# Sample queries stationary, keys copied, value products moved: the attention stage of a decoder step

## The chip, the cores and the metric

The kernel runs on one core of a Trainium2 chip. The metric is device time in microseconds of one execution, lower is better.

## The reference

One inference step of a one-layer hybrid decoder: 16 meta tokens and 256 prompt tokens, and 8 sample tokens with their caches, 280 rows of 1024 features. All in float32.

```python
h = rmsnorm(x, norm_mix)
xr, q, k, v, g_rnn, g_attn = split_in(h, w_in)         # 16 heads of 64, 2 kv heads
y_rnn = rg_lru(causal_conv(xr), w_rg, w_ig, lam)       # gates in 16 blocks of 64 x 64, a scan over the tokens
y_attn = window_attend(q, k, v, ...)                   # window 128, ALiBi slopes, a sink per head
x = x + concat(sigmoid(g_rnn) * y_rnn, sigmoid(g_attn) * y_attn) @ w_out
x = x + moe(rmsnorm(x, norm_ffn), ...)                 # top 4 of 32 experts, clamped SwiGLU
y = rmsnorm(x, norm_final)
...
# outputs: y, the last 128 keys and values, the convolution and scan states
```

The sample rows attend to their 127 cached keys and the new one, each row to its own cache.

## The kernel before, in words

Each engine runs a program written out by hand; order is that of the code, and semaphores tie the engines together. There are two stages.

**Trunk.** Everything is held feature-major: partitions are features, columns are the 280 tokens. TensorE goes through 34 projection blocks n (128 output features, eight matmuls over the 1024 inputs, line 1055): 0 and 1 are keys and values, 2 to 9 the recurrent branch, 10 to 17 the queries (BLK_Q), then the two sets of gates. Four PSUM banks and later two take the blocks in turn; ScalarE evacuates each (line 621). Between blocks TensorE does the small work:

- after_kv (line 939): keys and values are transposed to token-major, VectorE copies them (token_major, line 1445) into kt4, with each key head twice, and vt. keys_major (line 947, after block 4) transposes the doubled keys back, so that kd holds each kv head's keys in both halves of the partitions; ScalarE evacuates them (line 645). The halves are needed since queries of two heads lie in the two halves.
- gates(j) (line 954), after block j + 3: four 64 x 64 matmuls in four quarters of the array into banks 4 and 5; ScalarE takes them with three sigmoids (gate_evacs, lines 625 and 629). VectorE's convolution of block j must come first, GpSimd multiplies behind them.
- From step 0 (st, block ATT = 15) on, head pairs j = 0 to 7: scores(j) at st = 2j+1 (line 914), the softmax on VectorE and ScalarE, p_transposes(j) at st = 2j+3 (line 923), pv(j), the value products, at st = 2j+4 (lines 934 and 936), and ScalarE's evacuation of pv(j) right after (line 712).
- The 16 prompt tokens of the third tile (last rows) and the 8 sample rows have products of their own: last_scores and sample_scores at st 9 (lines 981 and 972), sample_rows at st 11 (line 987; it turns the sample scores so that rows are (sample, head)), last_p and sample_p at st 14, sample_pv at st 15 (line 1007), last_pv at st 16 (lines 1017 and 1018).

Matmuls name their part of the array by the partitions of operands and output: 64-row operands use half of its rows, 64-partition outputs half of its columns, and so on. This is what "tile size" means here.

After step 18 follow eight output blocks (line 1100), the router, and the experts.

**Experts.** 16 pairs of experts, 12 weight loads of 2 MB each, through ten places of SBUF. SyncE issues them (lines 432 and 436) as places come free: the first wait for attn_gated and bias_step, that is for VectorE's last gating of attention outputs (line 1646) and the split of the expert biases (lines 1651 to 1657); some of the ten places belong to trunk weights and wait for output blocks (wout_used). TensorE does the pairs with lines 1319 and 1355.

```python
elif 4 <= st <= 2 * KB + 2:
    pv((st - 4) // 2)                                   # line 1069
...
if st >= 4 and st % 2 == 0 and st <= 2 * KB + 2:        # line 709, ScalarE
    jj = (st - 4) // 2
    eng.wait_ge(s.pv_done, jj + 1)
    act(m_t[:, KB + jj, 0:2 * P], bank[5][:, 0:2 * P], ACT.Copy).then_inc(s.pv_evac, 1)
```

## Time and profile before

| what | value |
| --- | --- |
| median of 3 runs | 1148.07 us (1147.6 to 1148.33) |
| profiled execution: span from first to last instruction | 1146.0 us |
| TensorE busy | 1113.5 us, 97% |
| VectorE, ScalarE, GpSimd busy | 311.8, 229.6, 34.0 us |
| HBM read | 436.00 MB, 383 GB/s over the span |
| granted TensorE clock, mean | 0.999 |

The profile is of one execution. Its own time outside the profiler isn't recorded; beside the span stands the median of the runs, 2.07 us above it. The trace gives for each instruction its engine, line, start and duration; matmuls overlap, so the time of a group is read from one group's start to the next one's. A float32 matmul shows as two records.

### The profile page before, as it was taken

The numbers are of one execution on the slowest core, as the hardware profiler recorded it, in microseconds if no ns is written. First come the engines' busy times: TensorE is split into PE (matmuls) and PEld (weight loads), VectorE is DVE, ScalarE is ACT, GpSimd is POOL, SyncE is SP. The second block draws the span as 40 slices with busy tenths as digits, with TensorE's granted clock in tenths as the row PEclk, the third lists the DMA queues.
The fourth block names the chain that finished last, engine by engine and source line by source line (L and its number), as shares of the span: only waits on it lengthen the run. The fifth ranks groups of instructions, "written<-read, shape, count | busy, mean of one in ns | idle before, by whom it ended". The sixth has DMA issues, their size and how long they took to land.

```text
span 1146.0 us, 14903 instructions
## 1 busy us (share of the span) xinstructions
PE 1113.5 (97%) x5772; PEld 493.6 (43%) x5772; DVE 311.8 (27%) x785; ACT 229.6 (20%) x642; POOL 34.0 (3%) x69
## 2 busy tenths in 40 slices
PE   8999999999999999999999999999999999999997
PEld 6687778844333424333333333323232323232432
DVE  5665544032131221212130312121213030312123
ACT  4564363422020202010101111111111101010103
POOL 0200012210000000000000000000000000000000
PEclk9999999999999999999999999999999999999999
DMA  9743636989999999999999999999999999999995
GB/s 350 265 153 111 187 112 265 426 350 421 427 428 426 426 427 428 428 428 428 427 428 428 430 429 428 427 428 429 429 429 427 427 428 429 429 427 427 426 427 238
DMA packets 40802, 437.90 MB, mean 382 GB/s; under 512 B 6720, under 2 KB 9040, under 8 KB 11072
## 3 DMA queue, kind: packets, MB, share of 16 engines
q1 hardware_dynamic: 40136, 435.65, 91.2%
q10 hardware_dynamic: 624, 1.68, 0.4%
q8 instruction: 28, 0.46, 0.2%
q14 instruction: 14, 0.11, 0.0%
HBM read 436.00 MB, written 2.41 MB: 383 GB/s over the span
## 4 chain that ended last, share of the span: by engine, by line
PE 69%; DMA 24%; DVE 3%; ACT 2%; issue 1%; DVEq 0%; SPq 0%; ACTq 0%
PE bank L1319 21%; DMA ring<-in_w_down 20%; PE bank L1355 19%; PE bank L1055 8%; PE bank L1100 5%; PE bank L1201 4%; DMA area<-in_w_down 3%; PE bank L1222 3%; PE bank L1150 2%; PE bank L1235 1%; PE bank L1198 1%; PE bank L1036 1%; PE bank L1225 1%; DVE area L1748 1%; PE bank L923 1%
## 5 line engine op out<-in xcount | busy, mean ns | idle before, releaser
L1319 PE MATMUL bank<-ring,area 128*64 128x512 f32 x1744 | 396.4, 597 | 9.1 <-DMA ring<-in_w_up 8.7
L1319 PEld LDWEIGHTS bank<-ring,area 128*64 128x64 f32 x1744 | 117.2, 136 | 261.8 <-issue 222.9
L1355 PE MATMUL bank<-ring,area 128*64 128x512 f32 x928 | 213.7, 599 | 7.5 <-DMA ring<-in_w_down 7.5
L1736 DVE TENSOR_TENSOR x_tok<-x_tok,bank 128x512 f32<-128x512 f32 x60 | 41.3, 688 | 328.0 <-PE bank L1222 328.0
L800 ACT ACTIVATE area<-area 128x256 f32<-128x256 f32 x64 | 26.7, 417 | 516.3 <-DVE area L1748 516.3
L1055 PE MATMUL bank<-ring 128*128 128x264 f32 (+1 forms) x512 | 121.7, 393 | 0.0
L1355 PEld LDWEIGHTS bank<-ring,area 128*64 128x64 f32 x928 | 62.4, 136 | 117.9 <-issue 102.7
L1055 PEld LDWEIGHTS bank<-ring 128*128 128x128 f32 x512 | 95.2, 190 | 21.3 <-issue 4.0
L1773 DVE TENSOR_TENSOR area<-area 128x1024 f32<-128x1024 f32 x15 | 18.4, 1225 | 211.3 <-ACT area L810 211.3
L1222 PE MATMUL bank<-area 128*128 128x512 f32 x128 | 71.8, 644 | 0.0
L1319 PE MATMUL bank<-area 128*64 128x512 f32 x304 | 69.2, 597 | 1.5 <-DMA area<-in_w_up 1.5
L1100 PE MATMUL bank<-area,ring 128*128 128x264 f32 x256 | 58.6, 387 | 0.0
L1201 PE MATMUL bank<-area,h_tok 128*128 128x128 bf16 x768 | 54.2, 219 | 0.0
L1100 PEld LDWEIGHTS bank<-area,ring 128*128 128x128 f32 x256 | 48.0, 190 | 8.8 <-issue 1.0
L810 ACT ACTIVATE area<-bank,vec 128x128 f32<-128x128 f32 x120 | 34.3, 369 | 82.5 <-PE bank L1201 82.5
L1201 PEld LDWEIGHTS bank<-area,h_tok 128*128 128x128 bf16 x768 | 48.9, 98 | 0.0
L1748 DVE TENSOR_SCALAR area<-bank 128x256 f32<-128x256 f32 x64 | 26.9, 420 | 74.1 <-PE bank L1319 74.1
L1222 PEld LDWEIGHTS bank<-area 128*128 128x128 f32 x128 | 19.1, 188 | 51.6 <-issue 51.6
L1319 PEld LDWEIGHTS bank<-area 128*64 128x64 f32 x304 | 20.5, 136 | 45.2 <-issue 39.2
L820 ACT ACTIVATE area<-bank 128x512 f32<-128x512 f32 x32 | 19.1, 597 | 80.9 <-PE bank L1235 80.9
L1198 PE MATMUL bank<-area,h_tail 72*128 72x128 bf16 x128 | 28.5, 223 | 0.0
L1752 DVE SCALAR_TENSOR_TENSOR area<-area 128x256 f32<-128x256 f32 x64 | 27.2, 425 | 2.2
(271 smaller groups left out, 702.6 us busy)
## 6 DMA issues: line engine op xcount, KB each, us to landing
ring<-in_w_up SPq DMA_DIRECT2D x103, 2048.0 KB, 34.3
ring<-in_w_down SPq DMA_DIRECT2D x51, 2048.0 KB, 33.9
area<-in_w_up SPq DMA_DIRECT2D x17, 2048.0 KB, 29.8
ring<-in_w_in SPq DMA_DIRECT2D x16, 1024.0 KB, 9.3
ring<-in_w_down SPq DMA_DIRECT2D x13, 1024.0 KB, 10.6
ring<-in_w_up SPq DMA_DIRECT2D x12, 1024.0 KB, 9.7
area<-in_w_down SPq DMA_DIRECT2D x5, 2048.0 KB, 34.3
ring<-in_w_out SPq DMA_DIRECT2D x8, 1024.0 KB, 5.0
```

Of the source, the lines that this page charges most:

```text
L800: act(sig[:, n % 2, :], glu[:, n % 2, :], ACT.Sigmoid, scale=ALPHA).then_inc(s.sig_ready, 1)
L810: ins = act(xe[:, j, :], bank[half][:, P * i:P * (i + 1)], ACT.Copy, scale=vec[:, NFF + j:NFF + j + 1])
L1055: m = mm(proj_bank(n)[:, 0:T - lo], w[:, k, P * (n % 2):P * (n % 2) + P], (xn if n == 2 else h_t)[:, k, lo:T], start=(k == 0), stop=(k == ...
L1100: mo = mm(bank[m % 2][:, 0:NT], w[:, k, :], m_t[:, k, N_META:T], start=(k == 0), stop=(k == 2 * KB - 1))
L1198: mm(out, h_tail[0:TRIO, P * j:P * (j + 1)], g_oh[0:TRIO, 2, :], start=True, stop=False)
L1201: m = mm(out, parts[:, t, i, P * j:P * (j + 1)], g_oh[:, t, :], start=False, stop=(t == 1 and i == 2))
L1222: m = mm(b[:, :], gw_t[:, lo:lo + P], yd[:, NB * c:NB * (c + 1)], start=True, stop=True)
L1319: m = mm(bank[2 * h + n][64 * e:64 * e + 64, :], xe[:, k, 64 * e:64 * e + 64], w[:, kk, e, NB * n:NB * (n + 1)], start=False, stop=(k == K ...
L1355: m = mm(bank[4 + c][64 * e:64 * e + 64, :], y_t[:, 4 * half + f, 64 * e:64 * e + 64], w[:, f, e, :], start=False, stop=(half == 1 and f = ...
L1736: eng.tensor_tensor(x, x, combined_bank(unit, last)[:, :], ALU.add).then_inc(s.added, 1)
L1748: eng.tensor_scalar(glu[:, n % 2, :], z[:, :, 0], LIMIT, None, ALU.min).then_inc(s.glu_ready, 1)
L1752: eng.scalar_tensor_tensor(out=lin[:, n % 2, :], in0=lin[:, n % 2, :], scalar=1.0, in1=glu[:, n % 2, :], op0=ALU.add, op1=ALU.mult).then_i ...
```

## The change

1. keys_major goes. kt4 holds each key head once, token_major makes four copies and not six. kd is filled from kv_t by copies: GpSimd the halves whose partitions are their own (kd_own), ScalarE the crossed ones (kd_ready).
2. gates run by the table GATES: pairs (0, 1), (2, 3), (4, 5) after blocks 4, 6 and 8, gates 6 and 7 after blocks 9 and 10 as before. Odd gates use banks 6 and 7. ScalarE's evacuations follow the same table.
3. pv(j) moves from st = 2j+4 to st = 2j+5, between scores(j+2) and p_transposes(j+1); pv(7) stays at st 18. ScalarE evacuates pv(j) at st = 2j+6, and pv(6) and pv(7) both at st 18.
4. sample_scores: the queries are the stationary operand, 32 columns for each of four column tiles (four samples by eight query heads, the rest of the 16 zero for the other kv head), the cached keys move. The result has its rows where the softmax wants them; sample_rows and VectorE's copy s_t go. VectorE lays the queries out with eight copies and not four. Sample rows are now ordered by (sample mod 4, sample div 4, head).
5. last_pv does its four matmuls of 128 rows first and then its four of 16 rows.

```diff
+GATES = ((), (), (0, 1), (), (2, 3), (), (4, 5), (6,), (7,))
...
-                    eng.wait_ge(s.kd_ready, 2)
...
-                    eng.wait_ge(s.kvtok_ready, 6)
+                    eng.wait_ge(s.kvtok_ready, 4)
...
+            eng.wait_ge(s.zeroed, 10)
+            eng.wait_ge(s.kv_evac, 1)
+            for kv in range(N_KV):
+                half = slice(64 * kv, 64 * kv + 64)
+                eng.tensor_copy(kd[half, kv, :], kv_t[half, 0, :]).then_inc(s.kd_own, 1)
+                eng.wait_ge(s.kd_own, kv + 1)
...
+                    eng.wait_ge(s.kv_evac, 1)
                     for kv in range(N_KV):
-                        eng.wait_ge(s.kd_tr, kv + 1)
-                        act(kd[:, kv, :], bank[6 + kv][:, 0:T], ACT.Copy).then_inc(s.kd_ready, 1)
-                if j >= 1:
-                    gate_evacs(j - 1)
+                        there, here = slice(64 - 64 * kv, 128 - 64 * kv), slice(64 * kv, 64 * kv + 64)
+                        act(kd[there, kv, :], kv_t[here, 0, :], ACT.Copy).then_inc(s.kd_ready, 1)
+                for i in GATES[j]:
+                    gate_evacs(i)
...
-                if st >= 4 and st % 2 == 0 and st <= 2 * KB + 2:
-                    jj = (st - 4) // 2
-                    eng.wait_ge(s.pv_done, jj + 1)
-                    act(m_t[:, KB + jj, 0:2 * P], bank[5][:, 0:2 * P], ACT.Copy).then_inc(s.pv_evac, 1)
+                if st >= 6 and st % 2 == 0 and st <= 2 * KB + 2:
+                    for jj in range((st - 6) // 2, (st - 4) // 2 if st < 2 * KB + 2 else KB):
+                        eng.wait_ge(s.pv_done, jj + 1)
+                        act(m_t[:, KB + jj, 0:2 * P], bank[5][:, 0:2 * P], ACT.Copy).then_inc(s.pv_evac, 1)
...
             def p_transposes(j):
+                if j == 0:
+                    eng.wait_ge(s.gate_evac, 3 * KB)
...
-                if j:
-                    eng.wait_ge(s.gate_evac, 3 * j)
+                if j > 1:
+                    eng.wait_ge(s.gate_evac, 3 * (j - 1))
+                elif j == 1:
+                    eng.wait_ge(s.kvtok_ready, 4)
...
-                qd = qdz.rearrange("p k (g b) -> p k g b", g=GROUP)
-                for b in range(B_S):
-                    m = mm(bank[4][:, N_HEADS * b:N_HEADS * (b + 1)], kc_t[:, b, :], qd[:, :, :, b], start=True, stop=True)
+                for g in range(2):
+                    for i in range(4):
+                        r = slice(32 * i, 32 * i + 32)
+                        m = mm(bank[4][r, 0:P], qdz[:, g, r], kc_t[:, 4 * g + i, :], start=(g == 0), stop=(g == 1),
+                               skip_group_check=True)
...
-                for kv in range(N_KV):
-                    v = slice(HEAD * kv, HEAD * (kv + 1))
-                    for p in range(2):
-                        o, r = slice(64 * p, 64 * p + 64), slice(64 * p, 64 * p + 64)
-                        mm(bank[4][o, 64 * kv:64 * kv + 64], vt[:, 1, v], pt_2[:, kv, r], start=True, stop=False)
-                        m = mm(bank[4][o, 64 * kv:64 * kv + 64], vt[0:TAIL_P, 2, v], pt_2[0:TAIL_P, 2 + kv, r],
-                               start=False, stop=True)
+                for n, t in ((P, 1), (TAIL_P, 2)):
+                    for kv in range(N_KV):
+                        for p in range(2):
+                            r = slice(64 * p, 64 * p + 64)
+                            m = mm(bank[4][r, 64 * kv:64 * kv + 64], vt[0:n, t, HEAD * kv:HEAD * (kv + 1)],
+                                   pt_2[0:n, kv + (t - 1) * N_KV, r], start=(t == 1 and kv == 0), stop=(t == 2),
+                                   skip_group_check=True)
...
-                {2: after_kv, 4: keys_major}.get(n, lambda: None)()
+                {2: after_kv}.get(n, lambda: None)()
...
                     if st < 2 * KB:
                         scores(st // 2)
+                    if st >= 5:
+                        pv(st // 2 - 2)
                     if st >= 3:
                         p_transposes(st // 2 - 1)
-                elif 4 <= st <= 2 * KB + 2:
-                    pv((st - 4) // 2)
+                elif st == 2 * KB + 2:
+                    pv(KB - 1)
```

How the instructions move. TensorE, blocks 3 to 6 of the trunk, before (1055 are projection blocks, 963 gates, 951 the transposes of the keys):

```order
L1055 MATMUL bank<-ring 128x280 x8
L963 MATMUL bank<-ring,h_tok 64x280 x4
L1055 MATMUL bank<-ring 128x280 x8
L951 MATMUL bank<-keep,area 128x128 x2
L951 MATMUL bank<-keep,area 128x24
L951 MATMUL bank<-keep,area 128x128 x2
L951 MATMUL bank<-keep,area 128x24
L963 MATMUL bank<-ring,h_tok 64x280 x4
L1055 MATMUL bank<-ring 128x280 x8
L963 MATMUL bank<-ring,h_tok 64x280 x4
L1055 MATMUL bank<-ring 128x280 x8
L963 MATMUL bank<-ring,h_tok 64x280 x4
```

and with the change (1063 are the projection blocks, 973 the gates):

```order
L1063 MATMUL bank<-ring 128x280 x16
L973 MATMUL bank<-ring,h_tok 64x280 x8
L1063 MATMUL bank<-ring 128x280 x16
L973 MATMUL bank<-ring,h_tok 64x280 x8
```

Two blocks stand together, then two gates; the key transposes are gone. TensorE, one head pair's turn in the attention part, before (914 scores, 923 transposes of probabilities, 934 and 936 value products):

```order
L914 MATMUL bank<-area,ring 128x128 x2
L914 MATMUL bank<-area,ring 128x256 x2
L923 MATMUL bank<-keep,area 128x128 x6
L1055 MATMUL bank<-ring 128x264 x8
L934 MATMUL bank<-area 64x256 x2
L936 MATMUL bank<-area 64x128 x2
L1055 MATMUL bank<-ring 128x264 x8
```

and with the change (927, 949 with 951, 938):

```order
L927 MATMUL bank<-area,ring 128x128 x2
L927 MATMUL bank<-area,ring 128x256 x2
L949 MATMUL bank<-area 64x256 x2
L951 MATMUL bank<-area 64x128 x2
L938 MATMUL bank<-keep,area 128x128 x6
L1063 MATMUL bank<-ring 128x264 x16
```

The value products stand where TensorE is away from the full array anyway. ScalarE, its last instructions of the trunk with their waits, before (706 evacuates transposed probabilities, 712 value products):

```order
L621 ACTIVATE ring<-bank 128x264 [waits proj_done]
L706 ACTIVATE area<-bank 128x384 [waits pv_done,pt_done]
L621 ACTIVATE ring<-bank 128x264 [waits proj_done]
L712 ACTIVATE area<-bank 128x256 [waits pv_done]
L743 ACT_TABLE_LOAD
```

and with the change (718 and 724):

```order
L629 ACTIVATE ring<-bank 128x264 [waits proj_done]
L718 ACTIVATE area<-bank 128x384 [waits pv_done,pt_done]
L629 ACTIVATE ring<-bank 128x264 [waits proj_done]
L724 ACTIVATE area<-bank 128x256 [waits pv_done] x2
L755 ACT_TABLE_LOAD
```

Both of the last two value products are now evacuated behind the last projection block.

## Rows read from the trace of the kernel before

**Rows 1.** Windows: us, busy of each engine (x instructions), granted clock, DMA share, GB/s.

```profile
235.00:240.00 5.00, 4.79 (x37) 2.47 (x37) 2.01 (x6) 2.70 (x6) 1.45 (x4) 1.00 0.64 269
...
250.00:255.00 5.00, 5.00 (x36) 2.26 (x36) 2.63 (x9) 0.00 (x0) 0.00 (x0) 1.00 1.02 426
```

**Rows 2.** Chain of work that ended last: start us, us, what.

```profile
399.56 7.02 PE bank L1319 x32
...
454.52 7.02 PE bank L1319 x32
...
790.60 39.28 DMA ring<-in_w_down
...
849.33 39.29 DMA area<-in_w_down
```

**Rows 3.** Waits of SyncE's queue, 150 to 330 us: total us, times, longest.

```profile
SPq L436 <- PE bank L1100: 15.0, 2, 7.9
SPq L441 <- DVE bias_parts L1657: 13.3, 1, 13.3
```

**Rows 4.** TensorE's timeline, first probability transposes: start us, us, line, operation [idle before].

```profile
89.00 0.92 PE L923 MATMUL bank<-keep,area 128*128 128x128 f32 x6 [0.43 <-DVE area L1553]
```

**Rows 5.** TensorE's timeline, trunk blocks, key transposes and gates.

```profile
28.82 1.09 PE L951 MATMUL bank<-keep,area 128*128 128x128 f32 x6
29.84 0.70 PE L963 MATMUL bank<-ring,h_tok 64*64 64x280 f32 x8
30.48 4.04 PE L1055 MATMUL bank<-ring 128*128 128x280 f32 x16
...
35.08 4.04 PE L1055 MATMUL bank<-ring 128*128 128x280 f32 x16
...
57.88 21.66 PE L1055 MATMUL bank<-ring 128*128 128x264 f32 x96
```

**Rows 6.** Timelines of ScalarE, VectorE and GpSimd beside the gates.

```profile
25.25 1.28 ACT L625 ACT_TABLE_LOAD   x1
...
35.98 1.01 ACT L629 ACTIVATE ring<-bank,vec 64x280 f32<-64x280 f32 x2
...
35.60 0.50 DVE L1481 SCALAR_TENSOR_TENSOR ring<-ring,vec 128x272 f32<-128x272 f32 x1 [1.67 <-ACT ring L638]
...
37.37 0.74 DVE L1483 SCALAR_TENSOR_TENSOR ring<-ring,vec 128x8 f32<-128x8 f32 x1
...
28.15 0.77 POOL L545 TENSOR_TENSOR ring<-ring 128x280 f32<-128x280 f32 x1 [25.62 <-ACT ring L629]
```

**Rows 7.** Timelines of TensorE and VectorE, one turn of the attention part.

```profile
99.53 3.73 PE L1055 MATMUL bank<-ring 128*128 128x264 f32 x16
...
107.75 0.93 PE L914 MATMUL bank<-area,ring 64*128 64x128 f32 x8
...
109.32 3.73 PE L1055 MATMUL bank<-ring 128*128 128x264 f32 x16
...
104.82 0.34 DVE L1553 TENSOR_SCALAR area<-area 128x256 f32<-128x256 f32 x1
```

**Rows 8.** TensorE's timeline, sample scores and sample value products.

```profile
119.91 1.94 PE L972 MATMUL bank<-area,h_tok 128*128 128x16 f32 x16
121.70 3.81 PE L1055 MATMUL bank<-ring 128*128 128x264 f32 x16
...
151.72 1.10 PE L1007 MATMUL bank<-area 128*64 128x8 f32 x32
```

**Rows 9.** TensorE's timeline, the last rows' value products, first and the block behind.

```profile
157.21 0.28 PE L1017 MATMUL bank<-area 128*64 128x64 f32 x2
...
159.21 3.83 PE L1055 MATMUL bank<-ring 128*128 128x264 f32 x16
```

**Rows 10.** ScalarE's timeline, the last block and the last value products.

```profile
167.29 0.39 ACT L621 ACTIVATE ring<-bank 128x264 f32<-128x264 f32 x1 [3.40 <-PE bank L1055]
168.10 0.38 ACT L712 ACTIVATE area<-bank 128x256 f32<-128x256 f32 x1 [0.42 <-PE bank L936]
```

More of the change, by code:

```diff
@@ L356, in msk, with gate_banks @@
             return masks[:, lo - C_KEEP:lo - C_KEEP + n]
+        def gate_banks(j):
+            return bank[4 + 2 * (j % 2)], bank[5 + 2 * (j % 2)]
         def proj_bank(n):
@@ L623, in gate_evacs @@
             def gate_evacs(j):
+                r_bank, i_bank = gate_banks(j)
                 eng.wait_ge(s.gate_done, 2 * j + 1)
-                act(a_t[:, j, :], bank[4][:, 0:T], ACT.Sigmoid, bias=vec[:, BR + j:BR + j + 1]).then_inc(s.gate_evac, 1)
+                act(a_t[:, j, :], r_bank[:, 0:T], ACT.Sigmoid, bias=vec[:, BR + j:BR + j + 1]).then_inc(s.gate_evac, 1)
                 eng.wait_ge(s.gate_done, 2 * j + 2)
@@ L628, in gate_evacs @@
                     here, there = slice(64 * h, 64 * h + 64), slice(64 - 64 * h, 128 - 64 * h)
-                    act(b_t[there, j, :], bank[5][here, 0:T], ACT.Sigmoid, bias=vec[here, BI + j:BI + j + 1])\
+                    act(b_t[there, j, :], i_bank[here, 0:T], ACT.Sigmoid, bias=vec[here, BI + j:BI + j + 1])\
                         .then_inc(s.gate_evac, 1)
@@ L688, in _ @@
                 if n == BLK_Q:
-                    gate_evacs(KB - 1)
+                    for i in GATES[KB]:
+                        gate_evacs(i)
                 elif n < BLK_Q + 3:
@@ L945, in after_kv @@
                     tr.then_inc(s.kv_tr, 1)
-            def keys_major():
-                eng.wait_ge(s.kvtok_ready, 6)
-                for kv in range(N_KV):
-                    for t, (lo, n) in enumerate(TILES):
-                        tr = eng.transpose(bank[6 + kv][:, lo:lo + n], kt4[0:n, t, P * kv:P * (kv + 1)], ident[0:n, 0:n])
-                    tr.then_inc(s.kd_tr, 1)
             def gates(j):
@@ L962, in gates @@
                         c, half = h if g == 0 else 1 - h, slice(64 * h, 64 * h + 64)
-                        m = mm(bank[4 + g][64 * c:64 * c + 64, 0:T], wg[half, g, j, :], xc[half, j, :],
+                        m = mm(gate_banks(j)[g][64 * c:64 * c + 64, 0:T], wg[half, g, j, :], xc[half, j, :],
                                start=True, stop=True, tile_position=(64 * h, 64 * c))
@@ L982, in last_scores @@
                            start=True, stop=True)
-            def sample_rows():
-                eng.wait_ge(s.dsc_ready, 1)
-                eng.wait_ge(s.x_biased, 2)
-                eng.transpose(bank[4][:, 0:P], s_t, ident).then_inc(s.dst_done, 1)
             def sample_p():
@@ L1057, in _ @@
                 m.then_inc(s.proj_done, 1)
-                {2: after_kv, 4: keys_major}.get(n, lambda: None)()
+                {2: after_kv}.get(n, lambda: None)()
                 if BLK_XR + 1 <= n < BLK_Q + 1:
-                    gates(n - BLK_XR - 1)
+                    for j in GATES[n - BLK_XR]:
+                        gates(j)
                 st = n - ATT
@@ L1448, in token_major @@
                     src = bank[6 + i][:, 0:3 * P].rearrange("p (t k d) -> p t k d", t=3, k=N_KV)
-                    for dup in range(2 - i):
-                        dst = (kt4.rearrange("p t (k r d) -> p t k r d", k=N_KV, r=2)[:, :, :, dup, :] if i == 0
-                               else vt.rearrange("p t (k d) -> p t k d", k=N_KV))
-                        eng.tensor_copy(dst[:, 0:2], src[:, 0:2]).then_inc(s.kvtok_ready, 1)
-                        eng.tensor_copy(dst[0:TAIL, 2], src[0:TAIL, 2]).then_inc(s.kvtok_ready, 1)
+                    dst = (kt4, vt)[i].rearrange("p t (k d) -> p t k d", k=N_KV)
+                    eng.tensor_copy(dst[:, 0:2], src[:, 0:2]).then_inc(s.kvtok_ready, 1)
+                    eng.tensor_copy(dst[0:TAIL, 2], src[0:TAIL, 2]).then_inc(s.kvtok_ready, 1)
             def softplus():
@@ L1618, in _ @@
                         for p in range(2):
-                            eng.tensor_copy(qdz[64 * kv:64 * kv + 64, kv, :].rearrange("p (i r b) -> p i r b", i=4, r=2)[:, :, p, :],
-                                            q_t[64 * p:64 * p + 64, 4 * kv:4 * kv + 4, L:T]).then_inc(s.qd_ready, 1)
+                            for g in range(2):
+                                own = qdz[64 * kv:64 * kv + 64, g, :].rearrange("p (b h) -> p h b", b=4)
+                                h = N_HEADS * g + GROUP * kv + p
+                                eng.tensor_copy(own[:, h:h + GROUP - 1:2, :],
+                                                q_t[64 * p:64 * p + 64, 4 * kv:4 * kv + 4, L + 4 * g:L + 4 * g + 4])\
+                                   .then_inc(s.qd_ready, 1)
                     attention_sum(j)
```

23 lines of the change are left out of this document (10 added, 13 removed).

## The prediction

> **What bounds the kernel now.** I read four views. First the windows: between 250 and 255 us TensorE is busy all the time and the DMA engines are too, at 426 GB/s, while between 235 and 240 us they move only 269 GB/s [rows 1]. The reader should see that the transfers dip once, where the expert stage begins. Second the chain of work that ended last: until about 730 us an expert pair costs TensorE 54.95 us (454.52 - 399.56 = 54.96), later it repeats every 58.73 us (849.33 - 790.60) and each turn ends on a weight transfer [rows 2]. So the weight stream is the slower of the two from its start; TensorE only works off its lead. Third the waits of the DMA queue between 150 and 330 us: its first expert load waits 13.3 us for VectorE's bias pieces (the chain attention outputs, gating, bias split), and the eleventh, in two halves, waits 15.0 us for TensorE's last output blocks [rows 3]. Fourth TensorE's timeline: before the expert stage it has no idle time worth naming after 15 us except 0.43 us before the first probability transposes [rows 4].
>
> Put together: the end is the time at which the stream becomes steady plus a fixed amount of bytes. That time hangs on TensorE's output blocks and first expert loads, which hang on TensorE's own trunk. A microsecond taken from TensorE before 168 us therefore moves the end by one microsecond, as long as VectorE's attention chain (which releases the first loads) moves as well. No later cover hides it: TensorE's spare time after 730 us is of no use, but the stream's start is.
>
> **The change part by part.** The profiled span is 1146.0 us and the median of the runs 1148.07, so 2.07 us lie around the span; I treat them as fixed and subtract from the median.
>
> 1. **Key transposes out.** Line 951's six transposes go: 29.84 - 28.82 = 1.02 us [rows 5]. The keys are now copied inside SBUF: ScalarE makes two half copies in place of two from PSUM, about the same, and GpSimd two more near 18 us, in a stretch where it waits (25.62 us before 28.15) [rows 6], long before the first scores. VectorE loses two copies (about 0.5 us) before its second convolution. SP's wait for kvtok_ready 4 in place of 6 and the dropped kd_ready wait can only release it earlier. **-1.0.**
>
> 2. **Gates in pairs.** A projection block with its gates repeats every 35.08 - 30.48 = 4.60 us. A block alone takes 21.66/6 = 3.61 us for 264 columns, so 3.83 for 280; the gates cost 0.77. One matmul of 280 columns streams in 3.83/8 = 0.48; the four gate matmuls lie in four quarters of the array and can run side by side, so 0.48 is work and about 0.29 is the change of tile size there and back [rows 5]. Three visits go: **-0.9** (bounds 0 and -0.9).
>
> 3. **What pairing makes late.** ScalarE's gate evacuations (0.50 us each, three for a gate) now come six in a row, the first time with the 1.28 us table load and the two key copies in front. Block 4 ends near 28.1 us in the new order (28.82 less the gates that leave block 3). From there I add 0.2 for the signal, four copies of 0.45 (the block's two and the keys'), 1.28 and 6 x 0.50: 34.4 us before block 5's evacuation, and 1.0 more until its convolution can start, which took 2.5 us on VectorE (35.60 to 38.11): 37.9. TensorE, with 3.9 us for a block and 1.25 for a pair of gates, wants it for gates(3) at 37.5. The later pairs follow a block that had no gates in front of it, with 0.7 us to spare by the same sum. I take **+0.25** (0 to 0.5) [rows 6].
>
> 4. **Value products between scores and transposes.** A turn of two blocks lasts 109.32 - 99.53 = 9.79 us. Two blocks alone are 2 x 3.61 = 7.22, scores and transposes 109.32 - 107.75 = 1.57: the value products account for 1.00, of which 384 columns' streaming, 0.65, is work (their two halves lie side by side) [rows 5, 7]. The other 0.35 is at most 0.17 for each of two changes of tile size; rows 9 say 0.14. Between scores (64-row tiles) and transposes (full array) only one more change is needed. Six heads' pairs: 6 x 0.14 = **-0.8** (0 to 6 x 0.35 = -2.1). pv(6) is counted in 6. Nothing new is late: VectorE's next pt copy waits 0.4 us for the later transposes, and the probabilities, ready at 105.16, are wanted after the scores that start at 107.75.
>
> 5. **Sample scores with queries stationary.** Eight matmuls now cost 121.70 - 119.91 = 1.79 us, 0.11 per weight load record, for almost no columns. The new ones stream 8 x 128 columns in four column tiles: 0.22 us each, two rounds of four, 0.44 if they run side by side as the value products do, 1.75 if not. Small stationary tiles load fast here: the sixteen sample value matmuls took 1.10 us for 32 records. With two changes 0.75: **-1.0** (0 to -1.3). The rows' transpose (about 0.15, a sixth of the 0.92 us of six [rows 4]) and VectorE's copy go too, **-0.1** [rows 8]. VectorE's four more query copies, some 0.2 us each, lie where over 3 us are spare [rows 7].
>
> 6. **Last rows by tile size.** Eight matmuls alternate between 128-row and 16-row tiles: 159.21 - 157.21 = 2.00 us, 0.25 each, of which 64 columns stream in 0.11: 0.14 per change, the best single price of a change here [rows 9]. Grouped, two rounds of each kind take 4 x 0.11, and with the change between them 0.58. But pv(6) no longer stands in front in the same tile size, so it needs two changes of its own and this group one more: 0.28 to 0.42. 2.00 - 0.58 - 0.42 = **-1.0** (-0.6 to -1.4).
>
> 7. **The last value products wait.** This is the added wait. pv(7) stays after the last block and needs pv(6)'s bank evacuated. ScalarE did that a block earlier; now its order is evacuation of block 33, then pv(6), then pv(7). The first takes 0.39, the second 0.38, and a signal of about 0.1 lies ahead of and behind them: TensorE stands about 0.95 us before pv(7). Behind it on TensorE is the first output block; VectorE waits for the same evacuation with the last two gatings (before: 167.29 and 168.10) and then the bias split that releases the first loads [rows 10]. **+0.95** on both chains.
>
> Sum: -1.0 - 0.9 + 0.25 - 0.8 - 1.0 - 0.1 - 1.0 + 0.95 = -3.6 us. Both chains end on TensorE's last blocks, so the first loads and the first expert pair move together and the dip of rows 1 keeps its shape. 1148.07 - 3.6 = **1144.5 us**.
>
> Against the change speaks a rule of the Trainium skill (SBUF — State Buffer, Terms): VectorE and GpSimd share a port pair, and the loser "fully blocks". By that rule GpSimd's two key copies hold VectorE's normalizing and first convolutions up by their own length; taking one of its full products of 280 columns (0.77 us) for the pair's bound, the stall of term 3 would grow to 1.0 and the sum be -2.85, 1145.2 us. No row before shows the collision, since GpSimd waits in that stretch.
>
> **The rivals.**
>
> *Changes of tile size are not the cost* (13%). If the 0.14 to 0.29 us beside the streaming belong to weight loads or issue, which move along, terms 2, 4 and half of 6 vanish: -1.0 - 1.0 - 0.1 - 0.5 + 0.95 + 0.25 = -1.4, so 1146.7. For it: each of those matmuls has a weight load of its own. Against: rows 9, where the same small matmuls cost 0.25 alternating, and 16 sample matmuls in one tile size only 0.07 each [rows 8].
>
> *The scan chain keeps its time* (8%). The 0.43 us idle before the first transposes shows that ScalarE's and VectorE's chain from gates(7) to the first probabilities already ends last there. If the pairs delayed gates(7)'s evacuation by what TensorE gained (terms 1 to 3, 1.65 us), TensorE would wait that much longer and the time is 1148.07 - 1.95 = 1146.1. Against: gates 6 and 7 stay single, and the last pair's six evacuations (3.0 us) end before the next block does.
>
> *Everything at its good bound* (15%): terms 2, 4, 5 and 6 at -0.9, -2.1, -1.3, -1.4, no stall in 3: -1.1 - 0.9 - 2.1 - 1.3 - 1.4 + 0.95 = -5.85, so 1142.2.
>
> *Slower: TensorE's clock falls after the new pause* (4%). The 0.95 us stand before pv(7) follows small tiles. If the granted clock went from 2.4 to 1.2 GHz for one output block (16 matmuls, twice the 3.61 us of a projection block [rows 5]), that block would take 7.2 us more: 1144.5 + 7.2 = 1151.7. It decides once more than half an output block runs at the lower level. Against: the granted clock is 1.00 in the windows, also around the dip, where TensorE had short waits. The Trainium skill (TensorE: Matmul & The Clock Gate, Part 1) has the throttled state as the default that activity releases; by that rule the time is this rival's, if the pause is enough, and no row here shows one that was.
>
> **How the numbers follow.** The forecast itself has 60%, with 1143.4 to 1145.7 as its own range (terms 3 to 6 between neighbouring bounds). From the cases: faster by over 0.2% (below 1145.8; about what a measurement of this kernel can tell from no change) is the forecast and the good bound, 75%; within 0.2% the two rivals with 1146.7 and 1146.1, 21%; slower 4%. The range of 8 in 10 reaches from 1142.7 to 1146.8: it takes in the two rivals and most of the way to the good bound, and leaves out the slower case and the tails.
>
> **What would show it.** In the profile after: no transposes of keys; block pairs with gates about 0.3 us shorter per pair; turns of two blocks near 9.65 us; sample scores under 0.8 us; the last rows near 0.6 us; an idle time of about 0.9 us before the last value products, ended by ScalarE; the first expert load near 177.4 us and not 181.0, and the last weight landing near 1115. A wait of TensorE for the convolution at the second gate pair over 0.5 us makes term 3 wrong; sample scores near 1.8 us makes term 5 wrong. The whole is wrong if TensorE reaches the first output block 3.6 us earlier and the end does not follow, or if a granted clock below 1.00 appears.

## The result, and the profile after

The changed kernel takes 1150.24 us (median of 14 runs), the kernel before on the same chip 1147.52 us (14 runs): a ratio of 1.002, 95% interval 1.0012 to 1.0028. The change makes the kernel 2.7 us slower, where 3.6 us less were forecast. One of the 14 runs of the changed kernel was a slow one, 2902.27 us, and is left out of the ratio (the median without it is 1150.19). The profiled execution took 1150.52 us, with a span of 1148.7 us and a mean granted clock of 0.985 (before 1146.0 us and 0.999).

The trunk did what was forecast, and a little more. TensorE's timeline of the changed kernel, in the places of [rows 5], [rows 7], [rows 8] and [rows 9] (start us, us, line, operation, idle before it and what ended it):

```profile
20.25 7.71 PE L1063 MATMUL bank<-ring 128*128 128x280 f32 x32
27.89 1.18 PE L973 MATMUL bank<-ring,h_tok 64*64 64x280 f32 x16
28.99 7.81 PE L1063 MATMUL bank<-ring 128*128 128x280 f32 x32
36.74 1.28 PE L973 MATMUL bank<-ring,h_tok 64*64 64x280 f32 x16
37.95 7.81 PE L1063 MATMUL bank<-ring 128*128 128x280 f32 x32
...
97.26 7.29 PE L1063 MATMUL bank<-ring 128*128 128x264 f32 x32
...
106.85 7.29 PE L1063 MATMUL bank<-ring 128*128 128x264 f32 x32
...
117.33 0.64 PE L983 MATMUL bank<-h_tok,area 128*32 128x128 f32 x16
117.90 7.39 PE L1063 MATMUL bank<-ring 128*128 128x264 f32 x32
...
152.18 0.83 PE L1025 MATMUL bank<-area 128*64 128x64 f32 x16
152.94 3.83 PE L1063 MATMUL bank<-ring 128*128 128x264 f32 x16
...
162.78 0.65 PE L949 MATMUL bank<-area 128*64 128x256 f32 x4 [0.85 <-ACT area L724]
163.23 0.42 PE L951 MATMUL bank<-area 128*64 128x128 f32 x4
163.58 6.72 PE L1109 MATMUL bank<-area,ring 128*128 128x264 f32 x29
```

A pair of gates stands for 28.99 - 27.89 = 1.10 us (the second for 37.95 - 36.74 = 1.21), a turn of two blocks lasts 106.85 - 97.26 = 9.59 us instead of 9.79 [rows 7], the sample scores take 0.57 us instead of 1.79, the last rows 0.76 instead of 2.00, and the new wait is there with 0.85 us. The first output block starts at 163.58 us (before 167.99), the first expert matmul at 233.04 (before 237.44), and the first expert load is issued at 176.61 us (before 181.02): 4.4 us earlier, all three.

Then it is lost again. The page of the changed kernel, the lines that differ: the granted clock, the queue over which code is fetched, and the chain of work that ended last.

```profile
PEclk9999999999999999989999989999999999999999
...
q8 instruction: 55, 0.90, 0.3%
...
PE 90%; DVE 4%; issue 3%; ACT 2%; DMA 0%; DVEq 0%; SPq 0%; ACTq 0%
```

Before, q8 had 28 packets and 0.46 MB, and the chain was TensorE 69%, DMA 24%. TensorE's waits in the changed kernel (us in total, times, longest):

```profile
PE bank L1328 <- issue: 8.7, 3, 3.3
PE bank L1159 <- issue: 8.4, 3, 3.1
```

Neither row is in the answer for the kernel before, whose longest waits there are for weights. They fall at three places, about 504, 679 and 854 us. TensorE's timeline at the first of them:

```profile
500.48 3.65 PE L1364 MATMUL bank<-ring,area 128*64 128x512 f32 x16
506.85 1.03 PE L1159 MATMUL bank<-bias_parts,chosen 96*128 96x512 bf16 x4 [2.71 <-issue]
507.81 1.12 PE L1328 MATMUL bank<-area 128*64 128x512 f32 x1
512.21 6.08 PE L1328 MATMUL bank<-area 128*64 128x512 f32 x14 [3.28 <-issue]
```

L1159 are bias matmuls, here those with which a pair begins. TensorE's code for twelve of the sixteen pairs is a loop of three pairs, run four times; each of the three places is its jump back. TensorE waits twice for no other engine and no weight, and the windows around it (us, busy of each engine, granted clock, DMA share, GB/s) show that the work behind, 14 records in 6.08 us where 16 take 3.65 elsewhere, runs at a lower clock:

```profile
500.00:510.00 10.00, 6.22 (x31) 2.03 (x29) 1.83 (x3) 2.23 (x6) 0.00 (x0) 0.89 1.01 428
510.00:520.00 10.00, 7.79 (x24) 3.23 (x25) 0.00 (x0) 0.00 (x0) 0.00 (x0) 0.60 0.99 418
...
513.00:515.00 2.00, 2.00 (x8) 0.94 (x6) 0.00 (x0) 0.00 (x0) 0.00 (x0) 0.50 1.02 434
```

In windows of 2 us the granted clock is 0.50, the lower level of 1.2 GHz, from 509 to 517 us: it fell between 507 and 509 (0.69), behind the first wait, and came back between 517 and 519 (0.75), while TensorE worked.

In every third pair the bias matmuls ahead of its second half start at 264.91, 429.87, 604.80, 779.34 and 953.95 us: 164.96 us for three pairs without a jump, 174.93, 174.54 and 174.61 with one. Each jump back costs 9.6 to 10.0 us in this kernel, 29.2 together.

### The profile page after: what moved, and what is told of

Same layout as the page of the kernel before. It is cut to its first block, busy times and chain, and to the rows that moved or that the text cites. A ratio compares the mean times of both kernels' runs of the same rounds, so it can differ in the third digit from the quotient of the medians.

```text
span 1148.7 us, 14892 instructions
## 1 busy us (share of the span) xinstructions
PE 1116.1 (97%) x5765; PEld 496.5 (43%) x5765; DVE 310.8 (27%) x786; ACT 229.3 (20%) x642; POOL 34.6 (3%) x71
## 4 chain that ended last, share of the span: by engine, by line
PE 90%; DVE 4%; issue 3%; ACT 2%; DMA 0%; DVEq 0%; SPq 0%; ACTq 0%
PE bank L1328 36%; PE bank L1364 20%; PE bank L1063 8%; PE bank L1231 6%; PE bank L1109 5%; PE bank L1210 4%; PE bank L1159 2%; PE bank L1244 2%; PE bank L1234 1%; DVE area L1757 1%; DVE area L1769 1%; PE bank L1207 1%; PE bank L1044 1%; PE bank L938 1%; ACT area L812 1%
## 5 line engine op out<-in xcount | busy, mean ns | idle before, releaser
L1328 PE MATMUL bank<-area 128*64 128x512 f32 x304 | 79.6, 652 | 8.7 <-issue 8.7
L1328 PEld LDWEIGHTS bank<-area 128*64 128x64 f32 x304 | 24.7, 148 | 57.2 <-issue 56.9
L1159 PE MATMUL bank<-bias_parts,chosen 96*128 96x512 bf16 x96 | 27.8, 401 | 8.4 <-issue 8.4
```

Of the source, the lines that this page charges most:

```text
L1159: mm(bank[b0 + n - n0][:, :], chosen[:, :], bias_parts[:, NB * n:NB * (n + 1)], start=True, stop=False, skip_group_check=True)
L1328: m = mm(bank[2 * h + n][64 * e:64 * e + 64, :], xe[:, k, 64 * e:64 * e + 64], w[:, kk, e, NB * n:NB * (n + 1)], start=False, stop=(k == K ...
```

## The experiments

**Where the loop's code lies.** The program's instruction list says where this comes from. A transpose is two instructions, so the seven removed ones (six of keys, one of sample rows) put everything behind them 14 instructions earlier; the waits added and removed cancel. The loop is 1767 instructions long. With q8's 0.46 MB in 28 packets a fetch is 16.4 KB, and in the first pass through the loop (330 to 505 us) the kernel before makes seven, 252 instructions each. The Trainium skill (Runtime: NRT & Kernel Launch, Instruction fetch mechanics) gives pieces of 256 instructions, and a store of 2048 instructions for TensorE that is filled first in, first out. It also has a jump stall on a fetch when its target isn't in the current window of two pieces. The traces agree with the store and not with the window: in the kernel before each jump goes back over nearly seven pieces (1767 of 7 x 256 instructions), and q8 has no packet for it (below). Counted in pieces of 256, the loop begins at place 195 of its piece before the change and at 181 after (up to a constant: what is put ahead of the program when it is loaded isn't in the list). Theory A: at 181 the loop crosses one piece more, the store no longer holds it with the piece fetched ahead, and each jump back starts fetching all of it anew. Theories B and C were the rivals: the stalls come with the change's timing, or with its new pause and the clock.

a_plus14 gives the loop of the changed kernel its old place back, b_minus14 takes it from the kernel before, and a_plus40 and b_plus40 move both on by 40.

```diff
 a_plus14, changed kernel (a_plus40: 20 in place of 7; b_plus40: 20, in the kernel before)
             keep_warm(14, bank[7])
+            for _ in range(7):
+                mm(bank[7][:, 0:8], ones[:, :], ones[:, 0:1].to_broadcast([P, 8]), start=True, stop=True)
 b_minus14, kernel before
-            keep_warm(14, bank[7])
+            keep_warm(7, bank[7])
```

> Edit: the changed kernel with 7 matrix products of 8 columns (14 TensorE instructions) more in its warm-up, so that TensorE's loop over the expert pairs begins at the same place in its instruction stream as in the kernel before. Theory A (the place of the loop's code: moved 14 instructions towards the start, its 1767 instructions lie across one more 16 KB piece of the code, and at each of the three loop-backs the code is fetched again): no waits on issue of over 1 us in the expert stage, 28 packets on the instruction queue q8 as before the change, granted clock back at 1.00 per 100 us there, 1143.2 us, from 1142.5 to 1144.2 (1147.5 less the 4.4 us that the trunk gained). Theory B (the loop-back stalls come with the change's own timing: weights that arrive earlier, so that a fetch of code meets a fuller DMA, or TensorE comes to the loop-back in another phase): three stalls of some 6 us and 55 packets remain, 1149 to 1151 us. Theory C (the clock falls because of the 0.85 us pause ahead of the last value product, and the rest follows): clock 0.6 behind the loop-backs remains, 1148 to 1151 us.

> Edit: the changed kernel with 20 matrix products of 8 columns (40 TensorE instructions) more in its warm-up: the loop begins 26 instructions behind the place that it has in the kernel before. Theory A: 1767 instructions fit into seven pieces of 256 only from the first 26 places of a piece, so whatever the exact offset (unknown, since what the runtime puts ahead of the program is not in the program), this one lies across eight pieces again: three stalls, 55 packets on q8, 1149 to 1153 us. If instead seven or eight pieces make no difference and only the piece in which the loop's first instruction lies counts, no stalls, about 1144. Theories B and C: stalls as in the changed kernel, 1149 to 1153 us.

> Edit: the kernel before with 7 warm-up products instead of 14 (14 TensorE instructions less), nothing else: the loop begins where it does in the changed kernel. Theory A: three waits on issue of 2.5 to 3.5 us twice each at the loop-backs around 507, 682 and 857 us, 55 packets on q8, granted clock 0.6 for 10 us behind each; of some 30 us lost there, what the stream of weights doesn't hide remains: 1151 to 1157 us. Theories B and C: the kernel before has none of the change's timing, so no stall in its loop, 28 packets; 1147 to 1149 us, the later end for a colder clock at the start.

> Edit: the kernel before with 20 matrix products of 8 columns (40 TensorE instructions) more in its warm-up, nothing else. Theory A: offset over 25 in its piece of 256, so eight pieces, three stalls at the loop-backs, 55 packets on q8, 1151 to 1157 us. Theories B and C: 28 packets, no stall, 1147 to 1150 us (up to 2 us for the longer warm-up).

| kernel | loop begins at place | us (before 1147.74) | ratio, 95% interval | packets on q8 |
| --- | --- | --- | --- | --- |
| a_plus14 | 195 | 1143.29 | 0.9964 (0.9951 to 0.9978) | 28 |
| a_plus40 | 221 | 1143.39 (one run) | | 28 |
| b_minus14 | 181 | 1157.06 | 1.0084 (1.0069 to 1.01) | 55 |
| b_plus40 | 235 | 1153.43 (one run) | | 55 |

Fourteen instructions more, idle products of 0.3 us, take 7 us off the changed kernel (1150.24 to 1143.29, the profiled span from 1148.7 to 1140.8); fourteen fewer put 9.3 us on the kernel before. In a_plus14 TensorE has no wait on issue left, and the chain ends on the weights again; page and waits of **a_plus14**:

```profile
q8 instruction: 28, 0.46, 0.2%
...
PE 70%; DMA 24%; DVE 3%; ACT 2%; issue 1%; DVEq 0%; SPq 0%; POOL 0%; POOLq 0%
```

```profile
PE bank L1330 <- DMA ring<-in_w_up: 8.9, 35, 0.4
PE bank L1366 <- DMA ring<-in_w_down: 7.5, 11, 0.8
```

The longest waits of **b_minus14**, which has nothing of the change:

```profile
PE bank L1319 <- issue: 11.1, 3, 3.9
PE bank L1150 <- issue: 8.5, 3, 2.9
```

and of **b_plus40**:

```profile
PE bank L1152 <- issue: 10.9, 3, 3.7
```

So B and C fall: the stalls come and go with the place alone, in either kernel. One expectation of A fell with them. By the count 1767 instructions fit into seven pieces from 26 places in a row, and 195 and 221 are 26 apart, so at most one of them should have been free of stalls unless the count is off by one; both are. The runs bound the good stretch: at least the 27 places 195 to 221, and not 181 nor 235, so between one place in ten (27 of 256) and one in five (53); the kernel before stood on a good one. b_minus14 came out just beyond the end of its range since its colder start costs too: its output blocks start at 169.85 us, 1.9 later. So of its 9.3 us some 1.9 aren't the loop's.

What the place does to the fetches is seen in the queues' packets (queue: packets, MB, share). **Kernel before**, 330 to 505 us, the loop's first pass; in the next 175 us q8 has no packet at all:

```profile
q8 instruction: 7, 0.11, 0.3%
```

**Changed kernel**, 505 to 680 us, the second pass:

```profile
q8 instruction: 9, 0.15, 0.3%
```

Nine fetches in each of three passes are the 27 packets more. That agrees with the Trainium skill's first in, first out (same section): once the first piece is overwritten, each piece that is fetched drives out the next one needed.

The price of a jump depends on the place too. By the same bias matmuls it is 8.6, 8.9 and 9.1 us in b_minus14, and 5.4, 5.4 and 6.3 in b_plus40, which waits on issue once per jump and not twice.

**Is it the jump or the fetching?** Written out, the loop has nearly the same fetches and no jump.

```diff
 unrolled, on a_plus14
-            with eng.Fori(0, TURNS // (TRIPLE * PAIR_LOADS)) as it:
+            for it in range(TURNS // (TRIPLE * PAIR_LOADS)):
 peel_first: turn 0 written out, then Fori(1, ...); 40 small products in the warm-up
 peel_last:  Fori(0, ... - 1), then turn 3 written out
```

> Edit: the changed kernel (with the 14 warm-up instructions more) with TensorE's loop over the twelve middle pairs written out, so that TensorE takes no jump back; 5301 instructions more in the program, which are fetched in any case. Theory A, sharpened (a store of eight pieces of 256 instructions, one piece fetched ahead; what costs is a jump back to a piece that has been overwritten, not the fetching): about 28 + 21 = 49 packets on the instruction queue q8, nearly as many as in the changed kernel, but no wait on issue and no fall of the clock; 1143.3 us, from 1142.5 to 1144.3. Theory D (27 more code fetches of 16 KB disturb the weight stream or TensorE wherever they fall): 1146 to 1150 us, with waits on issue or on weights in the expert stage.

It took 1147.75 us (ratio 0.9999, 0.999 to 1.0009), with 48 packets on q8. A was half right and half wrong. The jump is what stalls TensorE: no wait on issue and no low clock is left. But twenty fetches aren't free. From the first expert matmul to the end the written-out kernel takes 1145.5 - 232.46 = 913.0 us, a_plus14 1140.8 - 232.18 = 908.6: 4.4 us. The time is in waits for weights, longest 2.0 and 1.2 us where a_plus14 has 0.8 and 0.4; waits of **unrolled**:

```profile
PE bank L1330 <- DMA ring<-in_w_up: 10.1, 36, 1.2
PE bank L1366 <- DMA ring<-in_w_down: 8.0, 10, 2.0
```

I took from this that a fetch costs something only from about 760 us on, where TensorE's lead is used up (theory E), and not wherever it falls (D). One turn written out, early or late, tells the two apart.

> Edit: the changed kernel with the first of the four turns of TensorE's loop written out ahead of the loop, and 40 products of 8 columns in the warm-up, so that the loop over the other three begins at place 200 of a piece of 256 (places 195 and 221 left no stall). Seven more pieces of code are fetched (35 packets on q8), all of them before 560 us, where TensorE keeps its full pace and the weights wait for it. Theory E (the fetches of the written-out kernel cost their 4.5 us where the stream of weights is the bound, from about 760 us on, since each holds up one weight transfer; before that they are free): no cost, 1143.6 us (1142.6 to 1144.6, the longer warm-up in it). Theory D (each extra fetch costs some 0.22 us wherever it falls): 7 x 0.22 = 1.6 us, 1145.

> Edit: the changed kernel with the 14 warm-up instructions more and the last of the four turns of TensorE's loop written out behind the loop: six or seven more fetches, between 760 and 940 us, where the weights are the bound. Theory E: waits for weights of over 1 us once or twice, 1145.3 us (1144.3 to 1147). Theory D: 1.6 us, 1144.9 (which this run alone doesn't tell from E; peel_first does). If neither, and the written-out kernel was slow for another reason (its jump-free waits, its fetches late in the program): 1143.3.

**peel_first**, with seven fetches more between 507 and 657 us, took 1144.78 us (0.9976, 0.9967 to 0.9985), **peel_last**, with six more between 843 and 976 us, 1144.53 (0.9975, 0.9966 to 0.9984). From the first expert matmul to the end that is 1142.7 - 233.04 = 909.7 and 1142.3 - 232.3 = 910.0 us, so 1.0 and 1.4 us more than a_plus14: 0.15, 0.23 and (unrolled) 0.22 us per fetch, early or late. D holds and E falls. In peel_first the early fetches cost late: from the bias matmuls at 264.91 us to those at 704.87 it is 0.2 us behind a_plus14, from there to those at 1114.32 another 0.9. The weight stream never pauses, and what a fetch takes from it is missed when the lead is gone. These differences are small, but the eight kernels with 28 packets all take 908.6 to 908.9 us for this stage. In peel_first the loop begins seven pieces later in the program, at place 200 of its piece, and doesn't stall either, so it is the place within a piece that counts. Why 16 KB, 0.04 us at 428 GB/s, cost four to six times that wasn't tried.

The kernels that stall have both costs, and the larger one decides. b_plus40 loses 5.4 + 5.4 + 6.3 = 17.1 us at its jumps, less than TensorE has to spare (21.5 us, worked out below), and from 945 us on it waits for weights again. Yet its expert stage takes 1151.6 - 237.15 = 914.5 us, 5.9 more than the kernel before: 0.22 us for each of its 27 fetches. b_minus14 is also 5.8 us longer there (1153.7 - 239.30 = 914.4). So the fetches alone would have taken back more than the trunk's 4.4 us (an estimate from these runs; no run has the changed kernel's fetches without its stalls).

**The trunk, part by part.** The start of the kernel varies by up to 1.0 us from one profile to another, so I measure from projection block 3 (which the expectations call the third) to the first output block. **Kernel before**:

```profile
20.38 3.94 PE L1055 MATMUL bank<-ring 128*128 128x280 f32 x16
...
167.99 4.27 PE L1100 MATMUL bank<-area,ring 128*128 128x264 f32 x18
```

That is 147.61 us before; 143.33 in the changed kernel, and 143.28, 143.29 and 143.30 in a_plus14, a_plus40 and unrolled. Each experiment below is an edit of a_plus14, with the loop at the same place.

```diff
 pv7_bank: the last value products in another PSUM bank
-                eng.wait_ge(s.pv_evac, j)
+                if j < KB - 1:
+                    eng.wait_ge(s.pv_evac, j)
+                vb = bank[5 if j < KB - 1 else 2]
 (and vb for bank[5] in the products and in ScalarE's copy)
 pairs_undone
-GATES = ((), (), (0, 1), (), (2, 3), (), (4, 5), (6,), (7,))
+GATES = ((), (0,), (1,), (2,), (3,), (4,), (5,), (6,), (7,))
 pv_back: pv((st - 4) // 2) at every even st from 4 on, ScalarE's copy in the same turn
 rows_undone: last_pv as before the change
 pv7_pair: pv7_bank, and the table's end (4, 5), (), (6, 7))
```

> Edit: the changed kernel with the 14 warm-up instructions more, and the last turn's value products written to PSUM bank 2, which is free by then, instead of bank 5, so that they don't wait for ScalarE's copy of the product before. If the 0.85 us wait at 162.8 us is a term of its own (+0.95 in the forecast): the first output block starts 0.8 us earlier, 1142.5 us against 1143.3. If ScalarE's copy, not TensorE, sets the end of the attention stage there: the wait moves to the output block's wait for the gated rows, 1143.3 us.

> Edit: the changed kernel with the 14 warm-up instructions more, and each turn's value products back in their own place behind the second projection block of the turn, with ScalarE's copy one turn earlier as before the change; the wait of the last products for the copy goes with it. By the forecast (-0.8 for eight turns, +0.95 for the wait): 0.15 us faster than 1143.3, 1143.15. By the trace of the changed kernel (0.20 less in each of seven turns, 0.85 wait): 0.55 us slower in the turns less 0.85, so 1143.0 (1142.7 to 1143.4). If tile-size changes cost nothing: 0.85 faster, 1142.45.

> Edit: the changed kernel with the 14 warm-up instructions more, and the gates one at a time again, one behind each projection block of the stage. By the forecast's terms (pairs save 0.9, ScalarE's double turn costs 0.25): 0.65 us slower than 1143.3, so 1143.95 (1143.6 to 1144.3); by the trace of the changed kernel (stage shorter by 1.96, of which the key transposes 1.0): 0.96 slower, 1144.25. Rival: switches between products of 128 rows and of 64 cost nothing, and the stage was shortened by the banks in turn: 1143.2 to 1143.4.

> Edit: the changed kernel with the 14 warm-up instructions more, and the sixteen-row queries' value products back in their order before the change (two products of 128 rows and of 16 rows in turn, four times). By the forecast's term 6: 1.0 us slower, 1144.3; by the trace of the changed kernel: 1.24 slower, 1144.5, and 1.24 more from the third projection block to the first output block (143.28 with the change). Rival (changes of tile size aren't what cost time): no more than 0.2 slower, 1143.3 to 1143.5.

Each ratio is to the kernel before on the same chip, whose medians are 1147.57 to 1147.99 us.

| kernel | us | ratio to before, 95% interval | block 3 to output block |
| --- | --- | --- | --- |
| a_plus14 | 1143.29 | 0.9964 (0.9951 to 0.9978) | 143.28 |
| pv7_bank | 1142.71 | 0.9953 (0.9939 to 0.9967) | 142.37 |
| pv_back | 1143.37 | 0.9959 (0.9943 to 0.9975) | 143.13 |
| pairs_undone | 1144.99 | 0.9974 (0.9963 to 0.9984) | 144.72 |
| rows_undone | 1144.51 | 0.9974 (0.9964 to 0.9984) | 144.60 |

*pv7_bank*: the wait is gone, and nothing took its place, 0.91 us. In the timeline of **pv7_bank** the products follow the block with no idle time:

```profile
158.72 3.28 PE L1066 MATMUL bank<-ring 128*128 128x264 f32 x14
161.93 0.65 PE L952 MATMUL bank<-area 128*64 128x256 f32 x4
162.41 0.39 PE L954 MATMUL bank<-area 128*64 128x128 f32 x4
162.73 6.50 PE L1112 MATMUL bank<-area,ring 128*128 128x264 f32 x28
```

*pv_back* has no such wait either, so against pv7_bank it is the place of the value products alone: 0.76 us. The seven moved products don't share this evenly. **pv_back**, from the block after the first transposes to the block before pv(6), and from there to the last block:

```profile
87.83 3.73 PE L1065 MATMUL bank<-ring 128*128 128x264 f32 x16
...
149.62 3.83 PE L1065 MATMUL bank<-ring 128*128 128x264 f32 x16
...
159.10 3.73 PE L1065 MATMUL bank<-ring 128*128 128x264 f32 x16
```

and **pv7_bank**:

```profile
87.75 7.29 PE L1066 MATMUL bank<-ring 128*128 128x264 f32 x32
...
148.40 3.83 PE L1066 MATMUL bank<-ring 128*128 128x264 f32 x16
...
158.27 3.73 PE L1066 MATMUL bank<-ring 128*128 128x264 f32 x16
```

Six turns are 61.79 - 60.65 = 1.14 us shorter with the move, 0.19 each; pv(6), which had stood beside the last rows' products of the same tile size, costs 9.87 - 9.48 = 0.39. The expectation from the trace had 0.20 for all seven and took the wait off twice, so it missed. Against a_plus14 its trunk is 0.15 us shorter, as the forecast's terms had it, and its time 0.1 us longer, which these intervals can't tell from 0.15 shorter. The move was thus worth almost nothing with the wait that it brought.

*pairs_undone* is 1.44 us longer in the trunk, more than the 0.96 expected. Of this 0.37 is a wait that only this kernel has, for the first convolution, since gate 0 now comes a block earlier. Timeline of **pairs_undone**:

```profile
20.33 3.94 PE L1065 MATMUL bank<-ring 128*128 128x280 f32 x16
24.64 0.70 PE L975 MATMUL bank<-ring,h_tok 64*64 64x280 f32 x8 [0.37 <-DVE ring L1492]
25.27 4.04 PE L1065 MATMUL bank<-ring 128*128 128x280 f32 x16
```

The other 1.07 is the pairs' own: against pairs_undone the three pairs save 0.43, 0.27 and 0.36 us (blocks and gates together, in a_plus14). The rival without a price for changes of tile size (no more than 0.1 slower) falls.

*rows_undone* is 1.32 us longer. Part of its timeline, **rows_undone**, is again the pattern of [rows 9]:

```profile
151.99 0.33 PE L1027 MATMUL bank<-area 128*64 128x64 f32 x2
152.24 0.32 PE L1028 MATMUL bank<-area 16*64 16x64 f32 x2
...
153.78 0.32 PE L1028 MATMUL bank<-area 16*64 16x64 f32 x2
154.03 3.83 PE L1065 MATMUL bank<-ring 128*128 128x264 f32 x16
```

The same sixteen matmul records take 2.04 us alternating and 0.76 in the grouped order. There are seven changes of tile size inside the first and one inside the second, so 1.28 us can't be these alone at the 0.14 read before: 6 x 0.14 = 0.84. The remaining 0.44 is what the prediction had for products of one size running two at a time (4 x 0.11 in place of 8 x 0.11); no run tells the two shares apart. Its rival falls too.

**A version that beats both.** The pv7_bank kernel is one, and a fourth pair of gates adds to it.

> Edit: the kernel with the last value products in PSUM bank 2 (1142.71 us), and gates 6 and 7 as a pair too. If a pair saves 0.36 us of TensorE as the first three did, and ScalarE's double turn fits there: 1142.35 us, and 142.0 from the third projection block to the first output block (142.37 without). Rival: ScalarE has the last gates' activations and the decay work of the scan in the same turn, so that TensorE waits for a PSUM bank or VectorE's scores come later: no gain or up to 0.5 us slower, 1142.7 to 1143.2.

It took 1142.15 us (0.9954, 0.994 to 0.9967), with 142.02 us in the trunk: 0.35 less, as expected. The difference of 0.56 us in the medians is of the size of the spread of either kernel (1141.72 to 1142.51 against 1141.99 to 1142.93), and the ratios to before, 0.9954 and 0.9953, show none, so for this last step the trunk is the evidence. Against the kernel before it saves 5.4 us.

## Why the prediction was wrong

**What failed.** The step that failed is the first one, in "What bounds the kernel now": "the end is the time at which the stream becomes steady plus a fixed amount of bytes". The first load and the first expert matmul came 4.4 us earlier, and the end came 2.7 us later. The amount of bytes wasn't fixed, since 27 fetches of code came in, and above all TensorE became the bound: the sentence held while TensorE used less than the stream's time, and 29.2 us at the jumps are more than it had to spare. From 703.82 us to 1112.39 us a_plus14 needs 408.6 us for seven pairs. TensorE's own pace is 54.97 us for a pair and 57.2 for the last (1121.14 - 1063.93 in the changed kernel, where it waits for no weight), 387.0 together: 21.5 us to spare, 7.7 too few. Behind that the changed kernel takes 0.85 us less (27.56 against 28.41), since a_plus14 waits for its last weights. That gives 6.8; measured, the expert stage is 7.0 us longer (915.7 us in the changed kernel, 908.6 in a_plus14). No rival had it. The prediction said itself what would overthrow it, that TensorE reaches the output blocks earlier and the end does not follow, or that a granted clock below 1.00 appears, and both did. But it named no mechanism that could do it: the instruction list was read for order, not for length or place.

**The slower rival.** It asked for a clock that falls after the new pause. The pause is there (0.85 us) and costs its own length, 0.91, no more: the granted clock stays at 1.00 from 160 to 170 us. 1.2 GHz does appear, but at the waits of a jump back, 5.3 to 6.0 us in two pieces, at other places than the rival said.

**The terms**, by the trunk alone, where -3.6 was forecast and -4.3 came:

1. Key transposes, -1.0. From block 3 to block 11 [rows 5] the stage went from 37.50 to 35.54 us; pairs_undone, less its own wait, takes 36.58. Keys 0.92: right.
2. and 3. Pairs, -0.9, and the stall, +0.25: -0.65 together, -1.07 measured (0.43, 0.27 and 0.36, where 0.30 each was put down), and the only trace of a stall is 0.1 us (1.21 against 1.10 above). Both were sized too cautiously. The collision of VectorE and GpSimd is there, and small: beside GpSimd's two copies (1.29 us) VectorE's four normalizing products take 21.25 - 18.27 = 2.98 us, before 21.01 - 18.40 = 2.61. That is 0.37 us, as in pairs_undone (21.33 - 18.35). TensorE waits for none of it. The stall of 1.0 us that the shared port would have made, by the Trainium skill's SBUF — State Buffer (Terms), is not in the trace.
4. Value products, -0.8 for six heads: -1.14, 0.19 each and not 0.14. Right in kind, sized too cautiously.
5. Sample scores, -1.0 and -0.1. The sixteen records take 0.57 us, not 0.75: -1.2, beside 0.1 for the transpose.
6. Last rows, -1.0, with pv(6) in it: 2.00 before, 0.71 (154.78 - 154.07 in pv_back, behind pv(6)) and 0.39 for pv(6) after, so -0.9: right. The order of the eight alone is worth 1.32 (rows_undone).
7. The wait, +0.95: 0.91.

These sum to -0.9 - 1.1 - 1.1 - 1.3 - 0.9 + 0.9 = -4.4, against the 4.3 measured. With the loop at its old place the changed kernel is 4.5 us faster (1143.29 against 1147.74), inside the forecast's range. The mechanisms in the trunk held, three of their sizes (pairs, value products, sample scores) were too small, and the sign of the whole was wrong.

The rival that changes of tile size are not the cost is refuted by pairs_undone and rows_undone. The scan chain did move: the wait before the first transposes is 0.43 us as in [rows 4], now at 86.93 us. The stream's waits stand as in [rows 3]; SyncE's for VectorE's bias pieces is 14.2 us instead of 13.3.

## What to carry to other kernels

Where an engine's code has a loop of nearly the length that it can hold (here 1767 instructions), count its instructions and note where in its piece of code it begins, before and after every edit, including edits far ahead of it; if a change of a few instructions moves the time by several us, look at the number of packets on the instruction queue and at waits on issue first. Pad the code to compare edits at the same place, and measure an edit over the stretch that it touches: here 143.28 to 143.30 us in three kernels, when whole times scattered by 1 us. Writing the loop out removes the dependence on the place, but in this kernel, bound by its weight stream, each 16 KB fetched cost about 0.2 us of it, and the written-out kernel was no faster than the one before the change.

## What was not expected of the hardware

- A jump back to code that is no longer held cost 9.6 to 10.0 us in the changed kernel: 5.3 to 6.0 us in two waits of 2.6 to 3.3 us, and the rest at a granted clock of 0.50 for some us (mean 0.59 to 0.80 in the windows of 10 us that hold it). It cost 8.6 to 9.1 us in b_minus14, and 5.4 to 6.3 in b_plus40, with one wait of 3.6.
- Fourteen instructions decide over 7 us in one kernel and 9.3 in the other (1.9 of these by a colder start). Places 195 and 221 are good, 181 and 235 are not.
- A fetch of 16 KB beside a full weight stream costs 0.15 to 0.23 us of the end, not the 0.04 that its bytes come to, even if it falls where TensorE does not wait for weights. The cause stays open.
- Eight products of two row sizes take 2.04 us alternating and 0.76 grouped; six changes at 0.14 and four products beside others at 0.11 would make up the 1.28 us.
- Two GpSimd copies of 1.29 us beside four VectorE products lengthen these by 0.37 us together, not by the copies' length.
